# A position-bias table written once as one row, instead of once for each partition

## The reference

```python
# 8 query heads of width 64 over 2 key heads; WINDOW = BLOCK = 128, two blocks of queries
qi = np.arange(BLOCK)[:, None]
kj = np.arange(2 * BLOCK)[None, :]
dist = BLOCK + qi - kj
in_band = (dist >= 0) & (dist < WINDOW)
bias = rel_bias[t5_bucket(np.clip(dist, 0, None))]        # by head: (8, 128, 256)
scores = jnp.einsum('bnqhgd,bnkhd->bnhgqk', qb, kb) * (HEAD_DIM ** -0.5)
scores = jnp.where(mask, scores + bias, -1e30)
probs = softmax(concatenate([scores, sink]))[..., :-1]    # a sink logit for each head
out = jnp.einsum('bnhgqk,bnkhd->bnqhgd', probs, vb)
```

## Time and profile before

| | us |
|---|---|
| Median of 3 runs | 1134.2 (1133.84 to 1134.38) |
| The profiled execution | 1135.42 |
| Its span, first to last instruction | 1133.6 |
| TensorE busy | 1027.0 (91%), mean granted clock 0.974 |
| VectorE, ScalarE, GpSimd busy | 251.0, 102.4, 8.9 |
| Bytes moved | 431.55 MB, 381 GB/s over the span |

### The profile page before, as it was taken

The page is one execution under the profiler, slowest core; times in us unless marked ns, Lnnn a source line. Parts: engine busy times, 40 slices in busy tenths (PEclk is TensorE's granted clock), DMA queues, the critical chain, the costliest instruction groups (busy, mean ns, idle before and its releaser), DMA issues.

```text
span 1133.6 us, 11141 instructions
## 1 busy us (share of the span) xinstructions
PE 1027.0 (91%) x4831; PEld 480.8 (42%) x4831; DVE 251.0 (22%) x561; ACT 102.4 (9%) x226; POOL 8.9 (1%) x20
## 2 busy tenths in 40 slices
PE   5499999999999998989898998898998989898986
PEld 4388874543434342424242434243434333333332
DVE  2032112331313211203031212121212121212112
ACT  1032011200101000001010101000000000000002
POOL 1200000000000000000000000000000000000000
PEclk9799999899999999999999999999999999999999
DMA  8760794699999999999999999999999999999994
GB/s 246 199 230 1 263 429 171 264 429 427 427 428 427 428 428 426 428 430 427 428 427 429 425 429 428 426 430 427 426 430 426 427 429 427 428 428 426 429 422 173
DMA packets 43302, 431.55 MB, mean 381 GB/s; under 512 B 5479, under 2 KB 7196, under 8 KB 18932
## 3 DMA queue, kind: packets, MB, share of 16 engines
q1 hardware_dynamic: 39992, 427.58, 89.7%
q0 software_dynamic: 976, 2.63, 1.4%
q10 hardware_dynamic: 2284, 0.60, 0.2%
HBM read 428.17 MB, written 2.62 MB: 380 GB/s over the span
## 4 chain that ended last, share of the span: by engine, by line
PE 51%; DMA 47%; DVE 1%; SPq 1%; issue 0%; ACT 0%; DVEq 0%; ACTq 0%
DMA ring<-in_w_down 32%; PE bank L774 15%; PE bank L819 15%; DMA ring<-in_w_up 11%; PE bank L572 9%; DMA ring<-in_w_in 4%; PE bank L729 3%; PE bank L855 3%; PE bank L675 3%; PE bank L767 1%; PE bank L758 1%; PE bank L692 0%; PE bank L589 0%; SPq L293 0%; PE bank L615 0%
## 5 line engine op out<-in xcount | busy, mean ns | idle before, releaser
L774 PE MATMUL bank<-ring,z_buf 128*64 128x512 f32 x2048 | 466.8, 610 | 51.0 <-issue 28.0
L774 PEld LDWEIGHTS bank<-ring,z_buf 128*64 128x64 f32 x2048 | 155.6, 140 | 347.7 <-issue 347.7
L819 PE MATMUL bank<-ring,m_buf 128*64 128x512 f32 x1024 | 226.8, 595 | 9.7 <-DMA ring<-in_w_down 9.0
L819 PEld LDWEIGHTS bank<-ring,m_buf 128*64 128x64 f32 x1024 | 78.1, 137 | 135.3 <-issue 132.7
L572 PE MATMUL bank<-h_buf,ring 128*128 128x256 f32 x400 | 91.5, 385 | 16.5 <-DMA ring<-in_w_in 15.6
L1116 DVE TENSOR_SCALAR swi<-bank 128x256 f32<-128x256 f32 x64 | 27.2, 425 | 311.9 <-PE bank L774 306.9
L572 PEld LDWEIGHTS bank<-h_buf,ring 128*128 128x128 f32 x400 | 76.7, 193 | 28.0 <-DMA ring<-in_w_in 16.1
L729 PE MATMUL bank<-u_buf,h_buf 128*128 128x128 f32 x512 | 64.5, 281 | 0.1
L729 PEld LDWEIGHTS bank<-u_buf,h_buf 128*128 128x128 f32 x512 | 62.1, 198 | 0.2 <-issue 0.2
L510 ACT ACTIVATE swi<-swi 128x256 f32<-128x256 f32 x64 | 26.7, 417 | 389.1 <-DVE swi L1116 389.1
L855 PE MATMUL bank<-y,u_buf 128*128 128x512 f32 x128 | 59.2, 605 | 0.0
(11 more groups left out here) (169 smaller groups left out, 322.1 us busy)
## 6 DMA issues: line engine op xcount, KB each, us to landing
ring<-in_w_up SPq DMA_DIRECT2D x128, 2048.0 KB, 36.8
ring<-in_w_down SPq DMA_DIRECT2D x62, 2048.0 KB, 36.8
ring<-in_w_in SPq DMA_DIRECT2D x6, 2048.0 KB, 31.6
ring<-in_w_out SPq DMA_DIRECT2D x2, 2048.0 KB, 15.7
ring<-in_w_pool_proj SPq DMA_DIRECT2D x1, 2048.0 KB, 21.8
ring<-in_w_attn_proj SPq DMA_DIRECT2D x1, 2048.0 KB, 22.4
ring<-in_w_down SPq DMA_DIRECT2D x2, 1024.0 KB, 32.8
ring<-in_w_down SPq DMA_DIRECT2D x4, 512.0 KB, 11.0
```

The source lines that it names most:

```text
L774: ins = nc.tensor.matmul(up_banks[j][e * SLOTS:(e + 1) * SLOTS, :], xgT[:, k, e * SLOTS:(e + 1) * SLOTS], w[e].rearrange("p (k n) -> p k n ...
L819: ins = nc.tensor.matmul(down_banks[n][e * SLOTS:(e + 1) * SLOTS, :], hidT[:, k, e * SLOTS:(e + 1) * SLOTS], w[e], start=(k == 0), stop=(k ...
```

## The change

There are four edits, and no work is added or left out in the computation.

- `skew` is 8 rows of 384 instead of 128 times that. GpSimd writes it with one transfer of 12 KB, waits for it, and reads it back at once: partition p reads each head's row from entry p on (step one element). This stands before the four sums now, and was behind them.
- Partition p then holds the bias of query 127 - p. So the queries are laid down in falling order within their block of 128: ScalarE's copy into `qT` reads PSUM backwards in each block, and VectorE's copy into `attnT` turns the order back in the same way.
- ScalarE issues five of its seven loads (the pool weights, the sinks, the router's weights and bias, `g2x`) behind the squares and roots of x, not ahead of them.
- ScalarE runs one root on a constant (`warm`) before it waits for x.

```diff
--- before.py
+++ after.py
@@ -100,7 +100,7 @@
     w_in_d, w_up_d, w_down_d = w_in[0], w_up[0], w_down[0]
 
 
-    skew = nc.dram_tensor("skew", [P, HEADS, 3 * WINDOW], F32, kind="Internal").ap()
+    skew = nc.dram_tensor("skew", [HEADS, 3 * WINDOW], F32, kind="Internal").ap()
 
     with ExitStack() as ctx:
         def sb(name, shape, dt=F32):
@@ -391,8 +391,12 @@
                                     base=0, pattern=[[1, P]], channel_multiplier=-1).then_inc(consts, 1)
 
             pool.wait_ge(*emptied_at("bias_rows"))
-            src = bias_row.unsqueeze(1).broadcast_to([HEADS, P, 3 * WINDOW])
-            nc.gpsimd.dma_start(skew.rearrange("p h i -> h p i"), src).then_inc(skew_written, 16)
+            nc.gpsimd.dma_start(skew, bias_row).then_inc(skew_written, 16)
+
+            pool.wait_ge(skew_written, 16)
+
+            back = bass.AP(skew.tensor, 0, [[1, P], [3 * WINDOW, HEADS], [1, 2 * WINDOW]])
+            nc.gpsimd.dma_start(band, back).then_inc(band_loaded, 16)
 
             src = uT
             for step in range(NG):
@@ -404,40 +408,40 @@
                 nc.gpsimd.tensor_tensor(dst[:, step:NG, PAD:], src[:, step:NG, PAD:],
                                         src[:, step:NG, PAD - far:PAD + SEQ - far], ALU.add).then_inc(summed, 1)
                 src = dst
-            pool.wait_ge(skew_written, 16)
-            pitch = HEADS * 3 * WINDOW
-            back = bass.AP(skew.tensor, WINDOW - 1, [[pitch - 1, P], [3 * WINDOW, HEADS], [1, 2 * WINDOW]])
-            nc.gpsimd.dma_start(band, back).then_inc(band_loaded, 16)
 
 
         @block.scalar
         def _(act):
             act.dma_start(rel[0:N_BUCKETS, :], rel_bias).then_inc(bias_in_loaded, 16)
             act.dma_start(bmap, buckets).then_inc(bias_in_loaded, 16)
+
+            steps = [0]
+
+            def link(ins):
+
+                steps[0] += 1
+                ins.then_inc(act_step, 1)
+                act.wait_ge(act_step, steps[0])
+
+            act.wait_ge(consts, 3)
+            link(nc.scalar.activation(warm, eps, ACT.Sqrt))
+            for t in range(TT):
+                act.wait_ge(x_loaded[t], 16)
+                link(nc.scalar.activation(xr[:, t, :], acc[:, t, :], ACT.Square, accum_out=ss[:, t:t + 1]))
+                nc.scalar.activation(std[:, t:t + 1], ss[:, t:t + 1], ACT.Sqrt, bias=eps,
+                                     scale=1.0 / D).then_inc(std_ready, 1)
+
             act.dma_start(pwt, pool_w[0].rearrange("g c d -> c g d")).then_inc(pw_loaded, 16)
             act.dma_start(snk, sinks[0].partition_broadcast(P)).then_inc(sinks_loaded, 16)
             act.dma_start(w_rt, w_router[0].rearrange("(k p) e -> p k e", p=P)).then_inc(router_loaded, 16)
             act.dma_start(b_rt[:, :], b_router[0].partition_broadcast(P)).then_inc(router_loaded, 16)
             act.dma_start(g2x[:, :], norm2_g[0].rearrange("(p k) -> p k", p=P)).then_inc(g2x_loaded, 16)
 
-            steps = [0]
-
-            def link(ins):
-
-                steps[0] += 1
-                ins.then_inc(act_step, 1)
-                act.wait_ge(act_step, steps[0])
-
-            act.wait_ge(consts, 3)
-            for t in range(TT):
-                act.wait_ge(x_loaded[t], 16)
-                link(nc.scalar.activation(xr[:, t, :], acc[:, t, :], ACT.Square, accum_out=ss[:, t:t + 1]))
-                nc.scalar.activation(std[:, t:t + 1], ss[:, t:t + 1], ACT.Sqrt, bias=eps,
-                                     scale=1.0 / D).then_inc(std_ready, 1)
-
             for i in range(2):
                 act.wait_ge(unit_done, UNIT[f"q{i}"] + 1)
-                nc.scalar.mul(qT[:, 2 * i:2 * i + 2, :].rearrange("p k t -> p (k t)"), bank[UNIT[f"q{i}"] % 8][:, :],
+
+                nc.scalar.mul(qT[:, 2 * i:2 * i + 2, :].rearrange("p k (b q) -> p (k b) q", q=P),
+                              bank[UNIT[f"q{i}"] % 8][:, :].rearrange("p (b q) -> p b q", q=P)[:, :, ::-1],
                               HD ** -0.5).then_inc(emptied["act"], 1)
             for i in range(2):
                 act.wait_ge(unit_done, UNIT[f"pool{i}"] + 1)
@@ -1008,7 +1012,8 @@
             gated("gate_pool", KD - 1, KD - 1)
             for i in range(2):
                 b = unit(f"attn{i}")
-                empties(nc.vector.tensor_copy(attnT[:, 2 * i:2 * i + 2, :].rearrange("p k t -> p (k t)"), b[:, :]))
+                empties(nc.vector.tensor_copy(attnT[:, 2 * i:2 * i + 2, :].rearrange("p k (b q) -> p (k b) q", q=P),
+                                              b[:, :].rearrange("p (b q) -> p b q", q=P)[:, :, ::-1]))
             for c in range(KD):
                 gated("gate_attn", c, KD + c)
             def add_out(q):
```

More of the change, by code:

```diff
@@ L416, in _ @@
             act.dma_start(bmap, buckets).then_inc(bias_in_loaded, 16)
[L417 to L421, removed]
             steps = [0]
@@ L436, in _ @@
                                      scale=1.0 / D).then_inc(std_ready, 1)
+            act.dma_start(pwt, pool_w[0].rearrange("g c d -> c g d")).then_inc(pw_loaded, 16)
+            act.dma_start(snk, sinks[0].partition_broadcast(P)).then_inc(sinks_loaded, 16)
+            act.dma_start(w_rt, w_router[0].rearrange("(k p) e -> p k e", p=P)).then_inc(router_loaded, 16)
+            act.dma_start(b_rt[:, :], b_router[0].partition_broadcast(P)).then_inc(router_loaded, 16)
+            act.dma_start(g2x[:, :], norm2_g[0].rearrange("(p k) -> p k", p=P)).then_inc(g2x_loaded, 16)
             for i in range(2):
                 act.wait_ge(unit_done, UNIT[f"q{i}"] + 1)
-                nc.scalar.mul(qT[:, 2 * i:2 * i + 2, :].rearrange("p k t -> p (k t)"), bank[UNIT[f"q{i}"] % 8][:, :],
+                nc.scalar.mul(qT[:, 2 * i:2 * i + 2, :].rearrange("p k (b q) -> p (k b) q", q=P),
+                              bank[UNIT[f"q{i}"] % 8][:, :].rearrange("p (b q) -> p b q", q=P)[:, :, ::-1],
                               HD ** -0.5).then_inc(emptied["act"], 1)
```

## The result

| | before | changed |
|---|---|---|
| Median, first measurement | 1134.29 us (4 runs) | 1119.91 us (4 runs, 1119.44 to 1120.22) |
| Ratio | | 0.987, 95% interval 0.9859 to 0.9882 |
| All executions of this study | 1134.1 us (51, 1131.98 to 1136.56) | 1119.0 us (13, 1116.93 to 1120.22) |
| The profiled execution, its span | 1135.42, 1133.6 us | 1120.15, 1118.4 us |

The change gains 14.4 us in the first measurement, 15.1 us over all executions. 1116.3 us was forecast, with a range of 1114.0 to 1121.5. The time is inside, 3.6 us above the forecast.

The account below looks back on a forecast made before the run. The weight stream bounds the kernel from about 205 us, starting when TensorE sets it. Savings of 15.65 + 1.84 + 0.4 = 17.9 us, taken from the 1134.2 us median, gave 1116.3 us, range 1114.0 to 1121.5.

Parts of the forecast that it names:

- The wait for C_KV goes whole: TensorE's wait before the kv unit for a w_in load, 15.65 us, vanishes; the load lands at 19.8 us.
- No wait behind it: After C_KV, C_Q and the gate and projection loads land before TensorE wants them; bias and later small loads hidden: no cost.
- The read-back: GpSimd's one-element-step read of the table runs like the old one, 9.6 us to landing, and stays hidden.
- Rivals 1 and 2: Slow readback delays C_KV: at the write's rate 1127.0 us (8%); at half that rate, slower than before, 1148 us (3%).
- GpSimd's new wait costs nothing: Waiting for the small write before the four sums is covered by the u and kv units: 0 us.
- The clock after the gap: Without TensorE's gap, the 16 first kv matmuls take 3.51 us, not 5.35: 1.84 us gained.
- There is no idle time from 17.5 us on: TensorE works without a gap from 17.5 us, the reason for taking 1.84 us rather than 0 for the clock.
- the sign that u1 ends at 31.0 to 31.5 us: One of the signs listed as showing the forecast right: TensorE's u1 unit ends in that span.
- The front 0.4 us: At the start, x and the three vectors land 0 to 0.74 us sooner with five loads moved back; 0.4 us taken.
- Falling queries 0: Four copies reading PSUM backwards cost 0 at the same or double duration; 1.6 us at four times.
- The stream shifts whole: The expert weight stream starts when TensorE frees ring slots, so time saved before it reaches the end whole.
- rival 3: Another wait behind C_KV (backward reads at four times, C_Q, sums or bias late) returns some gain: 1119.7 us, 9%.

Follow-up runs that it names:

- the 14: Changed kernel plus 14 TensorE transposes of the identity between the bias rows and the transposes of x: 1115.19 us (5 runs); repeated, 1114.26 us (5 runs).
- the changed kernel's second set: The changed kernel measured again with nothing edited: 1117.45 us (5 runs), ratio 0.9852.

## Why the old write was slow

The forecast needed only that the write goes. Two kernels ask what was slow in it. Both are the kernel before with all its bytes: the 12 KB row goes out first, and the 1536 KB of copies are then written from device memory.

```diff
-            src = bias_row.unsqueeze(1).broadcast_to([HEADS, P, 3 * WINDOW])
-            nc.gpsimd.dma_start(skew.rearrange("p h i -> h p i"), src).then_inc(skew_written, 16)
+            nc.gpsimd.dma_start(row_d, bias_row).then_inc(skew_written, 16)
+            pool.wait_ge(skew_written, 16)
+            nc.gpsimd.dma_start(skew, bass.AP(row_d.tensor, 0, [[0, P], [3 * WINDOW, HEADS], [1, 3 * WINDOW]])).then_inc(skew_written, 16)
...
-            pool.wait_ge(skew_written, 16)
+            pool.wait_ge(skew_written, 32)
```

> The kernel before, but the 1536 KB table of 128 copies is written from a 12 KB row in device memory, not from the eight partitions; outermost dimension 128. The bytes written stay, 12 KB more go out first. Theory (the write was slow by its source, eight partitions of SBUF, and by the eight engines it used): the bulk write takes some 10 us and not 36 us, C_KV lands in time, time like the changed kernel's, 1117 to 1121. Rival (the bytes or the 1.5 KB rows into memory are what is slow): the write takes 25 us or more and most of the wait for C_KV stays.

One run: 1118.22 us. The write, KB and us to landing:

```profile
skew<-row_d POOLq DMA_DIRECT2D x1, 1536.0 KB, 9.5
```

The other one keeps the order of the transfer of before, the 8 heads outermost and 128 copies inside:

> As the kernel with the bulk write out of device memory, but with the 8 heads outermost in the transfer, as in the kernel before. It tells the number of engines from the source. Theory of the source (two doors of SBUF behind eight partitions): as fast as with 128 outermost, or at most twice as long, because eight engines do all of it: 8 to 16 us; C_KV in time. Rival (the number of engines and the order of the rows is what was slow): about 36 us again, half of the sixteen engines busy, C_KV late near 47 us, time 1133.

One run: 1119.05 us.

```profile
skew<-row_d POOLq DMA_DIRECT2D x1, 1536.0 KB, 16.3
```

36.0 us from the eight partitions, 16.3 us from memory in the same order (I had expected 8 to 16), 9.5 us with 128 outermost. The bytes and the 1.5 KB rows are not what was slow. More than half of the 36.0 us was the source, eight partitions of SBUF; 6.8 us of the other 16.3 us go with the outermost dimension of 8. The quicker write leaves SP's queue less while it lasts: from 20 to 26 us that queue moved 0.90 MB beside it, and 1.53 MB beside the other. And with all 1536 KB still written, both kernels have the changed kernel's time: C_KV lands in time in both, and u0, u1 and kv run without a gap. So the gain does not need the bytes saved.

What these two kernels do not separate is the source from the moment. The big write waits for the small one and is issued at 15.9 and 15.5 us, where before it was issued at 9.8 us, and its first packets come between 19 and 20 us, where they came behind 14 us before. SP's queue had moved 5.5 and 5.4 MB by 20 us, and C_KV is complete at 5.25 MB by the prediction's sum; it landed 21.8 and 18.6 us after its issue at 3.2 us. A write as slow as the old one, begun so late, would have met C_Q and not C_KV. No run has it.

## Why the prediction was right, and where its sum was off

- **The wait for C_KV goes whole: right.** 15.65 us; no wait for a w_in load is left in the changed kernel's profile. C_KV landed 15.9 us after its issue at 3.2 us, at 19.2 us; 19.8 us was forecast.
- **No wait behind it: right.** C_Q, the sums (VectorE takes them at 42.49 us, 3 us after they are ready), the bias (57.08 us) and the pool weights (8.3 us to landing) hold nothing up.
- **The read-back: right.** 10.1 us against the 9.6 us that I took from the old one. Rivals 1 and 2, a slow read, did not happen.
- **The old write's slowness laid to its eight source partitions alone: right in the main only.** Out of device memory in the same order it took 16.3 us, not 36.0, but 9.5 us with 128 outermost; one run each. The sum did not need it.
- **GpSimd's new wait costs nothing: right.** The write took 5.5 us; the sums start when u1 is copied, as before.
- **The clock after the gap: right, 1.84 us.** It is regained: the 16 matmuls of kv are at the higher level in all profiles of the changed kernel.
- **"There is no idle time from 17.5 us on", so no lower level: wrong.** This is the step that failed, a term that was left out of the sum. The lower level at the start had been in the kernel before as well, in its transposes (records of 421 ns, against 273 ns with the 14 ahead of them). In its u0 no profile shows it; with ScalarE's edits alone one does, under the wait for C_KV. I took u0 at the higher level from one profiled execution and read the clock's row, which says 1.00 there. It costs 2.40 us in the profile of the changed kernel and none in the profile of the changed kernel's second set. By it the sign that u1 ends at 31.0 to 31.5 us failed as well: VectorE could copy its bank only at 33.38 us.
- **The front 0.4 us: right by size.** u0 starts 0.59 us earlier, the vectors land 0.68 us sooner (6.54 against 7.22 us). The early root gave nothing that shows: std for t = 1 is ready at 8.0 us and VectorE takes it at 10.7 us.
- **Falling queries 0: right.**
- **The stream shifts whole: right in the first profile.** From the first product of the first expert pass to the end the profile of before has 923.6 us (1133.6 - 210.00) and the changed one 923.8 (1118.4 - 194.57). Of all fourteen profiles eleven have 923.5 to 923.9. Three have 925.5 to 925.7 (the changed kernel's second set and the two with the bulk write): in these TensorE is at the lower level (granted clock 0.57 to 0.60 over 4 us) behind the wait 28 us before the end, shown above. The stage between was taken to shift whole too; it took 88.5 us before and, by w_out's third quarter, 86.5 to 88.8 us in the profiles of the changed kernel.

With the sum mended: 0.59 + 15.65 + 1.84 - 2.40 = 15.68 us at the attention product, where 15.74 us were measured. In the second set, with the early rise, it came at 103.62 us, 17.88 us before the old 121.50: the forecast sum of 17.9. That the whole execution, at 1117.45 us, was also 18.0 us shorter than the old one is luck: 1.96 us gained between the attention product and the experts (88.50 to 86.54) and 1.94 us lost in the stream (923.6 to 925.54) cancel. The rest of the miss may be the base: I took 17.9 us from the median, and they were read from a profiled execution that was itself 1.2 us above it.

The time that rival 3 gave, 1119.7 us, is close to the result, but by none of its causes. It was not right.

## What to carry to other kernels

A wait on the critical path covers what lies ahead of it on the waiting engine. Before it is credited in full, ask what the engine does up to the wait in other executions too, not only in the profiled one. A copy out of a few partitions can be slow by its source: here 1536 KB out of eight partitions took 36.0 us. Write a small table once and let the reading pattern do the copying; here it steps by one element and overlaps itself, and the read took 10.1 us. Small loads ahead of the weights can cost more than their bytes, here 0.7 MB for 0.27. And when two total times agree with a sum, compare the stages too: two of them can differ and cancel.

## What the runs showed of the hardware

- The clock's rise at the start is not tied to the program: identical programs had it before u0 or about 5 us later, 1.8 to 2.4 us apart over 80 matmuls. The row of the granted clock says 1.00 in both; the spacing of the matmuls tells (0.22 or 0.44 us; records of 379 or 634 ns).
- Identical programs also differ in the clock behind short matmuls (16 matmuls of w_out in 8.56 or 6.87 us) and behind a wait of 2.1 us (32 matmuls in 8.79 or 7.09 us).
- A transfer from device memory whose 128 rows overlap, each one element further, ran as fast as one without overlap: 10.1 against 9.6 us for 1024 KB beside full traffic.
- Reading PSUM backwards cost nothing: 0.60 us on ScalarE and 0.69 us on VectorE for 128x512, as forwards.
- Two transfers of 1536 KB out of device memory: 16.3 us with an outermost dimension of 8, 9.5 us with 128; out of eight partitions of SBUF 36.0 us (one profile each, beside SP's stream).
